# A hybrid diffusion block on eight cores: a second norm taken tile by tile inside the output projection, paired adaLN units, and six smaller moves

## The chip, the cores and the metric

The kernel runs on the 8 NeuronCores of one Trainium2 chip. The cores don't talk to each other: each takes two context sequences and half of a latent sequence. Time is device time in microseconds of the slowest core; lower is better.

## The reference, cut to what matters

One layer with model width D = 2048, 8 heads with values of 128, and a feed-forward width of 4 D:

```python
sh1, sc1, g1, sh2, sc2, g2 = split(silu(c) @ w_ada + b_ada)   # c_ctx for context tokens
h = rms_norm(x, w1) * (1 + sc1) + sh1
q, k, v, u, g = split(h @ w_in)          # q, k normed per 64; rotary on latent tokens
a = softmax(q1 k1) - lam * softmax(q2 k2)
att = rms_norm(a @ v, subln_w) * (1 - lam_init)
sgu = gelu(u) * (w_s @ layer_norm(gelu(g)) + b_s)   # 128x128 mixing per group and chunk
x = x + g1 * (concat(att, sgu) @ w_o)
h = rms_norm(x, w2) * (1 + sc2) + sh2    # the second norm
x = x + g2 * (square(relu(h @ w_ff1)) @ w_ff2)
```

Latent queries attend to all 2048 latent keys of their sequence and 256 cached context keys, context queries to their own 256. Outputs are both token streams and the new keys and values of the context.

## The kernel before, in words

A core owns 1536 tokens, in 12 tiles of 128: tiles 0 to 3 are context, 4 to 11 latent. Tiles 12 to 19 are the other half of its latent sequence, for keys and values alone. A scheduler, `Sched.add`, keeps readers and writers of each named buffer and puts semaphore waits in; an engine does its instructions in the order in which the program emits them. GpSimd's queue issues the weight loads (they convert to bf16), SP's the loads and stores of x and the small constants.

**Front (lines 300 to 460).** Twelve tiles are normed and transposed, and 16 slabs of adaLN weights (shift and scale of the first norm; `ada1_dma`, `ada1_mm`) go through a ring of four buffers. Slab by slab (`acc0`) the first four projection blocks of head 0 build up. Then head 0 is filled (`fill(0)`), with the other half's tiles normed, transposed and modulated in between by the generator `oth_gen` (L817). Its first three loads wait for `("sa1", 12)`. The bias load of `badaT_t` is emitted ahead of them on SP's queue; its buffer overlays the ring of the 16 slabs.

**Attention (L858 to L894).** 8 heads of 38 steps. A step: two exponentials on ScalarE (L866), some units of the next head's fill, the scores of the next step (`s_mm`, L739), and the value matmuls (L885). A fill has 13 projection blocks of 8 units and one cache unit; for heads 1 to 7 each of the 8 q and k blocks is followed by an adaLN unit (`ada_unit`), one of 64 slabs of 128 columns. 56 stand in the fills, 8 in head 7's steps (`si % 4 == 2`). The first 32 give the second norm's shift and scale with the slab as the stationary side (L513, 2 columns stream, result 128 x 2). The 32 gate units have the slab as the moving side (L531, result 2 x 128), load a bias row and store a piece of a row to the DRAM tensor `gate_rows`. All of it uses one PSUM tile, `pm`, shared with the q/k norm's sum (L554), the key transposes (L579), the cache transposes (L661) and the transposes of the finished block (L796); `pm_use` emits the pending reader of pm before its next writer. Two clocks, `FP` for fills and `MP` for finished blocks, post work so many ticks ahead. After the last step both are flushed.

**Weights of head 1** ("W" in `order`) are asked for after the first block of `fill(0)`.

**u, g and the mix.** u (L955): 8 slabs, three groups of 512 tokens each, into `sguT` through gelu. g (L982, `g_tile`): 12 tiles, with gelu, layer norm (square root on ScalarE, so table loads) and the mix (L1007), which runs two tiles behind. The last two mixes, `late_mix`, stand in the first slab of the output projection, after its second and its fourth group.

**Halves (L1062 on).** Two halves of six tiles. Output projection: 8 column blocks `nb`, each one 16 x 256 weight slab in a ring `wb` of three, six groups of 16 matmuls (L1073). `fused_add` multiplies by the gate (L1058) and adds into `acc` (L1059), both on VectorE; ScalarE squares into partial sums (L1080). When all 48 groups are done, the second norm: `norm_a` (sum, square root, reciprocal, a scaling of the 2048-wide row, L1093), `norm_b` (16 transposes, L1104, and copies on ScalarE and VectorE, L1111 and L1113) and `modulate` (12 scalings on VectorE, L1124, 4 on ScalarE, L1121, for tiles 0 to 3 and for 4 and 5). The first feed-forward group waits for all 16 of tiles 0 to 3. Then four rounds of ff1 (L1145) and ff2 (L1162), 8 slabs each. In the last round of half 0, SP stores each column block and then loads the next half's x into the same place, before the stores of the next block:

```python
for i, (dst, a_, n_) in enumerate(ytile(half, nb)):
    A("sp", ..., key=("yout", nb, i))
if half == 0:
    A("sp", ... dma_start(out=acc[:, :, nb * 256:nb * 256 + 256], in_=rows(xtile(nb))),
      writes=[("acc", ti, nb) for ti in range(6)], key=("xin", nb))
```

Of the kernel before, what the change touches and what calls it, by code (L numbers as in the profile page):

```python
# [8 lines left out]
F32 = mybir.dt.float32  # L9
# [4 lines left out]
D = 2048  # L14
# [128 lines left out]
def build_program():  # L143
# [10 lines left out]
    cT = din("cT", [128, 32]); w_adaA = din("w_adaA", [16, 128, 16 * 256]); badaA = din("badaA", [128, 64]); w_adaB = din("w_adaB", [64, 128, 16 * 128]); badaT = din("badaT", [128, 64]); badaG = din("badaG", [2, 2, D])  # L154
# [28 lines left out]
def _body(nc, top, L):  # L183
    globals().update({k: v for k, v in L.items() if k not in ("nc", "top")})
    with top:
# [32 lines left out]
        nw2_t = sbt(top, "nw2_t", [128, 16])  # L218
        attT = sbt(top, "attT", [128, 8, NTOK], BF16)
# [23 lines left out]
        with ExitStack() as pf:  # L243
# [6 lines left out]
            ARENA = 50700  # L250
            arena = sbt(pf, "arena", [128, ARENA], BF16)
            if True:
# [21 lines left out]
                badaT_t = ar.take(64, F32)  # L274
# [5 lines left out]
                wa2 = Ring("wa2", [tk3(16, 128) for i in range(3)])  # L280
                mch = Ring("mch", [ar.take(128, F32)[0:2, :] for i in range(2)])
# [219 lines left out]
                def ada_unit():  # L501
# [3 lines left out]
                    ada_i[0] += 1  # L505
                    ci, j = k // 16, k % 16
                    wt, wr = ada_slots.pop(k)
                    if ci < 2:
                        dst = S2 if ci == 0 else A2

                        def mm(e):
                            for kc in range(16):
                                ins = e.matmul(pm[:, 0:2], lhsT=wt[:, kc, :], rhs=scT[:, kc, :], start=(kc == 0), stop=(kc == 15))  # L513
                            return ins
                        pm_use(lambda: A("pe", mm, reads=[wr, "scT"], writes=[pmr]),
                               lambda: A("dve", lambda e: e.tensor_tensor(out=dst[:, j, :], in0=pm[:, 0:2], in1=badaT_t[:, ci * 32 + 2 * j:ci * 32 + 2 * j + 2], op=ALU.add),
                                         reads=[pmr, "badaT_t"], writes=[("modc2", ci, j)]))
                        if k == 31:
                            def fin():
                                for r in range(2):  # L520
                                    A("dve", lambda e, r=r: e.scalar_tensor_tensor(out=A2[:, :, r], in0=A2[:, :, r], scalar=1.0, in1=nw2_t[:], op0=ALU.add, op1=ALU.mult),
                                      reads=[("modc2", 1, jj) for jj in range(16)] + ["nw2_t"], writes=[("modc2", 1, jj) for jj in range(16)])
                            FP.post(4, fin)
# [741 lines left out]
```

How the kernel before makes its waits and increments, by code:

```python
    def _wait(self, eng, sem_name, sem, val):  # L39
        if self.waited[eng].get(sem_name, 0) >= val:
            return
        self.eng[eng].wait_ge(sem, val)
        self.waited[eng][sem_name] = val
# [1 line left out]
    def add(self, eng, fn, reads=(), writes=(), key=None):  # L45
# [15 lines left out]
        ins = fn(self.eng[eng])  # L61
        node = _Node()
        node.eng = eng
        node.dma = key is not None
        if key is not None:
            name = "d_" + str(key)
            if name not in self.dsem:
                self.dsem[name] = self.es.enter_context(self.nc.semaphore(name))
                self.dcnt[name] = 0
            self.dcnt[name] += 1
            ins.then_inc(self.dsem[name], 16)
            node.signal = (name, self.dsem[name], 16 * self.dcnt[name])
        else:
            self.cnt[eng] += 1
            ins.then_inc(self.esem[eng], 1)
            node.signal = ("c_" + eng, self.esem[eng], self.cnt[eng])
        for r in reads:
            self.readers.setdefault(r, []).append(node)
```

## Time and profile before

| | us |
|---|---|
| median of 3 runs (2758.24 to 2761.27) | 2758.82 |
| the profiled execution | 2762.95 |
| its span on the slowest core, core 3 | 2761.7 |
| TensorE busy | 2511.8 (91%) |
| VectorE busy | 988.5 (36%) |
| ScalarE busy | 839.6 (30%) |
| GpSimd busy | 210.2 (8%) |
| mean granted TensorE clock, core 3 | 0.972 |

The profile is of one execution, on the slowest core. Busy is the time in which an engine had an instruction of its own. The granted clock is that of TensorE as a share of 2.4 GHz; 0.50 is 1.2 GHz. A timeline merges neighbouring instructions of one line and tile. Matmuls overlap, so a row's duration reaches some 0.1 us or more into the next row.

### The profile page before, as it was taken

What the parts mean: (1) busy time and instruction counts of PE and PEld (TensorE: products, weight loads), DVE (VectorE), ACT (ScalarE), POOL (GpSimd) and SP (SyncE); (2) the same over time, 40 slices, a digit from 0 to 9 for tenths busy, and PEclk for the clock granted to TensorE, in tenths of its full rate; (3) what the DMA queues carried; (4) which work ended last, traced back from release to release, by engine and by line L of the source; (5) the groups of instructions that cost most, each with busy time, mean ns of one, the idle gap of its engine ahead of it and who ended that gap; (6) DMA issues with size and microseconds to landing.
All of it is one profiled execution on the core that took longest, in us unless ns stands there. A gap on an engine that the chain in (4) does not pass through costs nothing.

```text
span 2761.7 us, 57540 instructions; the slowest of 8 cores (2743.7 to 2761.7 us)
## 1 busy us (share of the span) xinstructions
PE 2511.8 (91%) x22176; PEld 1776.4 (64%) x22176; DVE 988.5 (36%) x2447; ACT 839.6 (30%) x1685; POOL 210.2 (8%) x338
## 2 busy tenths in 40 slices
PE   1458999999998889988999999999989999999999
PEld 1345565565565544467687786867875776868768
DVE  1334443443343320565142241423443331413324
ACT  2335665665665541643101101010122001010010
POOL 0111111111111000000000000000000000000000
PEclk9969999999999999998999999999998999999999
DMA  9994334334423355154555555557983555555556
GB/s 201 187 213 84 63 64 77 62 56 76 73 46 57 62 106 107 22 138 77 92 101 99 107 98 102 104 98 134 174 181 62 104 98 106 98 102 107 95 110 149
DMA packets 82298, 282.43 MB, mean 102 GB/s; under 512 B 11632, under 2 KB 45040, under 8 KB 58480
## 3 DMA queue, kind: packets, MB, share of 16 engines
q0 software_dynamic: 43232, 226.87, 47.4%
q1 hardware_dynamic: 38800, 51.89, 5.9%
q8 instruction: 182, 2.98, 0.4%
q14 instruction: 84, 0.69, 0.1%
HBM read 488.78 MB, written 16.81 MB: 183 GB/s over the span
## 4 chain that ended last, share of the span: by engine, by line
PE 80%; DMA 6%; DVE 5%; ACT 4%; issue 4%; DVEq 0%; ACTq 0%; SPq 0%; POOLq 0%; POOL 0%
PE pg L1145 8%; PE pS L1145 8%; PE pO L1162 8%; PE pS L1162 8%; PE pg L1162 8%; PE pO L1145 8%; PE pO L885 5%; PE pg L623 4%; PE pS L739 3%; PE pg L640 2%; PE pT L623 2%; DMA arena<-xp 2%; PE pO L1073 2%; PE pS L1073 2%; PE pg L1073 2%
## 5 line engine op out<-in xcount | busy, mean ns | idle before, releaser
L866 ACT ACTIVATE arena<-pS 128x512 bf16<-128x512 f32 x578 | 312.9, 593 | 245.5 <-PE pS L739 239.5
L1150 DVE TENSOR_TENSOR arena<-arena 128x512 bf16<-128x512 bf16 (+1 forms) x256 | 91.9, 359 | 572.2 <-ACT arena L1149 572.2
L1059 DVE TENSOR_TENSOR hT_own<-hT_own,arena 128x256 f32<-128x256 f32 x480 | 204.3, 426 | 63.5 <-DMA hT_own<-xs 12.0
L885 PE MATMUL pO<-arena 128*128 128x129 bf16 x2432 | 198.1, 225 | 11.5 <-ACT arena L866 9.0
L885 PEld LDWEIGHTS pO<-arena 128*128 128x128 bf16 x2432 | 144.9, 100 | 76.2 <-issue 75.9
L1145 PE MATMUL pg<-arena 128*128 128x256 bf16 (+1 forms) x960 | 157.5, 322 | 0.0
L1145 PE MATMUL pO<-arena 128*128 128x512 bf16 (+1 forms) x896 | 157.0, 333 | 0.0
L1162 PE MATMUL pS<-arena 128*128 128x256 bf16 x1344 | 153.6, 273 | 0.0
L1162 PE MATMUL pO<-arena 128*128 128x256 bf16 x1344 | 153.6, 273 | 0.0
L1162 PE MATMUL pg<-arena 128*128 128x256 bf16 x1344 | 153.6, 273 | 0.0
L1149 ACT ACTIVATE arena<-pg 128x512 bf16<-128x512 f32 (+1 forms) x86 | 42.4, 493 | 351.3 <-PE pg L1145 351.3
L1149 ACT ACTIVATE arena<-pS 128x256 bf16<-128x256 f32 (+1 forms) x86 | 42.0, 488 | 348.7 <-PE pS L1145 348.7
L1149 ACT ACTIVATE arena<-pO 128x512 bf16<-128x512 f32 (+1 forms) x84 | 41.2, 491 | 345.0 <-PE pO L1145 345.0
L1162 PEld LDWEIGHTS pO<-arena 128*128 128x128 bf16 x1344 | 131.4, 98 | 15.4
L1162 PEld LDWEIGHTS pg<-arena 128*128 128x128 bf16 x1344 | 131.4, 98 | 15.3
L1162 PEld LDWEIGHTS pS<-arena 128*128 128x128 bf16 x1344 | 131.3, 98 | 15.4
L1145 PE MATMUL pS<-arena 128*128 128x256 bf16 (+1 forms) x832 | 136.0, 322 | 0.0
L1145 PEld LDWEIGHTS pg<-arena 128*128 128x128 bf16 x960 | 93.9, 98 | 59.1
L1145 PEld LDWEIGHTS pO<-arena 128*128 128x128 bf16 x896 | 87.7, 98 | 63.9
L623 PE MATMUL pg<-hT_own,arena 128*128 128x512 bf16 x464 | 121.5, 389 | 0.0
L739 PE MATMUL pS<-arena 64*128 64x256 bf16 x1156 | 115.9, 279 | 4.7 <-ACT arena L866 4.2
L1145 PEld LDWEIGHTS pS<-arena 128*128 128x128 bf16 x832 | 81.4, 98 | 50.8
(236 smaller groups left out, 3755.9 us busy)
## 6 DMA issues: line engine op xcount, KB each, us to landing
arena<-w_ff POOLq DMA_DIRECT2D x84, 1024.0 KB, 8.9
shr<-w_ff POOLq DMA_DIRECT2D x44, 1024.0 KB, 9.0
arena<-w_adaB POOLq DMA_DIRECT2D x64, 512.0 KB, 5.5
arena<-w_adaA POOLq DMA_DIRECT2D x16, 1024.0 KB, 21.6
arena<-xs SPq DMA_DIRECT2D x16, 1024.0 KB, 9.7
arena<-w_in POOLq DMA_DIRECT2D x32, 512.0 KB, 8.0
arena<-w_o POOLq DMA_DIRECT2D x12, 1024.0 KB, 11.5
hT_own<-xs SPq DMA_DIRECT2D x8, 768.0 KB, 12.3
```

What stands on the lines that cost most here:

```text
L623: ins = e.matmul(pt[:], lhsT=wt[:, kc, :], rhs=hTs(kc, tb * 512, 512), start=(kc == 0), stop=(kc == 15))
L640: ins = e.matmul(pt[:, u * 128:(u + 1) * 128], lhsT=hTs(kc, tb * 512 + u * 128, 128), rhs=wt[:, kc, :], start=(kc == 0), stop=(kc == 15))
L739: ins = e.matmul(bk[c][:, j * 256:j * 256 + 256], lhsT=kT[p][64 * c:64 * c + 64, (kt + j) * 128:(kt + j) * 128 + 128], rhs=qz[p][64 * c:64 ...
L866: A("act", lambda e, t=bk[c], P=P: e.activation(out=P, in_=t[:], func=AF.Exp, scale=0.125), reads=[bkr[c]], writes=[Pr])
L885: ins = e.matmul(pO[b][:, c * 130:c * 130 + 129], lhsT=Ps[c][0][:, j * 256 + b * 128:j * 256 + b * 128 + 128], rhs=vv[p][:, kt + j, 0:129] ...
L1059: A("dve", lambda e: e.tensor_tensor(out=acc[:, ti, c], in0=acc[:, ti, c], in1=tmp, op=ALU.add), reads=[tmr, ("acc", ti, nb)], writes=[("a ...
L1073: ins = e.matmul(pt[:, 0:256], lhsT=lt, rhs=wcol(wt, kc, 0, 256), start=(kc == 0), stop=(kc == 15))
L1145: ins = e.matmul(pt[:, 0:cn], lhsT=wcol(wt, kc, fj * 128, 128), rhs=h2T[:, kc, c0:c0 + cn], start=(kc == 0), stop=(kc == 15))
L1149: A("act", lambda e, pt=pt, rl=rl, cn=cn: e.activation(out=rl[:, 0:cn], in_=pt[:, 0:cn], func=AF.Relu), reads=[pr], writes=[rlr])
L1150: A("dve", lambda e, rl=rl, fc=fc, c0=c0, cn=cn: e.tensor_tensor(out=aT[:, fc, c0:c0 + cn], in0=rl[:, 0:cn], in1=rl[:, 0:cn], op=ALU.mult) ...
L1162: ins = e.matmul(pt[:, 0:256], lhsT=aT[:, fc, ti * 128:(ti + 1) * 128], rhs=wcol(wt, fc, 0, 256), start=(fc == 0), stop=(fc == 15))
```

## The change

- adaLN units come in pairs, after every second q or k block of a fill, and in head 7 at steps 4, 10, 16 and 22. All 64 have the slab as the stationary side. Gates collect in `gcol`, are transposed once and stored in one DMA. The slab ring has four buffers.
- The flush after the last attention step goes; its posted steps run during u, two ticks of each clock per group. `wsb` and `bsb` are loaded after u's fourth slab.
- The late mixes stand after the fifth group of the first and of the second slab of the output projection.
- The second norm of tile ti - 1 runs beside the nb 6 and nb 7 groups of tile ti, for which two weight slabs are held. Square root and reciprocal become Ln and Exp. The first feed-forward group is in four quarters, each waiting for four of the 16 rows, with the last two tiles' transposes between quarters. For nb 6 and 7 the add of `fused_add` is on GpSimd.
- In the last round of half 0, x of block nb - 1 is loaded after the stores of block nb. The last store is three.
- The other half's first loads wait for `("sa1", 14)`; the weights of head 1 are asked for after k3.

```diff
-                        for kc in range(16):
-                            ins = e.matmul(pm[0:2, 0:128], lhsT=scT[:, kc, :], rhs=wt[:, kc, :], start=(kc == 0), stop=(kc == 15))
...
+                        for u in range(2):
+                            for kc in range(16):
+                                ins = e.matmul(pm[:, 2 * u:2 * u + 2], lhsT=sl[u][0][:, kc, :], rhs=scT[:, kc, :], start=(kc == 0), stop=(kc == 15))
...
+                    for kk in (k + 4, k + 5):
+                        if kk < 64:
+                            FP.post(4, lambda kk=kk: ada_dma(kk))
...
-                        order = ["v1", "W", "v2", "v0", "C", "k0", "q0", "k3", "v3", "k4", "V", "v4"]
+                        order = ["v1", "v2", "v0", "C", "k0", "q0", "k3", "W", "v3", "k4", "V", "v4"]
...
-                            yield from ada(1)
+                            nb_ += 1
+                            if nb_ % 2 == 0:
+                                yield from ada(1)
...
-                FILL_UNITS = 8 * 13 + 1 + 8
+                FILL_UNITS = 8 * 13 + 1 + 4
...
-                    ld = [x_load(t, reads=[("sa1", 12)]) for t in range(12, 15)]
+                    ld = [x_load(t, reads=[("sa1", 14)]) for t in range(12, 15)]
...
-                        if si % 4 == 2:
+                        if si % NS in (4, 10, 16, 22):
                             ada_unit()
...
-                MP.flush()
-                FP.flush()
-                while ada_i[0] < 64:
-                    ada_unit()
-                    FP.flush()
...
+                    for _ in range(2):
+                        MP.tick()
+                        FP.tick()
...
+                if gi == 3:
+                    MP.flush()
+                    FP.flush()
...
+                for nb in range(6):
+                    wt, wr = pend_w.pop(0)
+                    for ti in range(6):
+                        o_group(nb, ti, wt, wr)
+                        if late_mix and ti == 4:
+                            late_mix.pop(0)[1]()
+                    w_more()
...
+                w67 = [pend_w.pop(0), pend_w.pop(0)]
+                na = {}
                 for ti in range(6):
...
+                    o_group(6, ti, *w67[0])
+                    if ti >= 1:
+                        norm_a1(ti - 1)
+                    if ti >= 2:
+                        norm_b(ti - 2, *na[ti - 2])
                     if ti == 5:
                         modulate(0)
...
+                    o_group(7, ti, *w67[1])
+                    if ti >= 1:
+                        na[ti - 1] = norm_a2(ti - 1)
+                norm_a1(5)
+                na[5] = norm_a2(5)
+                w_more()
+                w_more()
+                tail_norm = [lambda: norm_b(4, *na[4]), lambda: norm_b(5, *na[5]), lambda: modulate(1)]
...
+                            if rd == 0 and fb == 0 and c0 == 0 and fj == 0:
+                                for k4 in range(0, 16, 4):
...
+                                    A("pe", mm4, reads=[wr] + [("h2T", kc, 0) for kc in range(k4, k4 + 4)], writes=[pr])
+                                    if k4 in (4, 12):
+                                        tail_norm.pop(0)()
+                                tail_norm.pop(0)()
...
-                                A("sp", lambda e, nb=nb: e.dma_start(out=acc[:, :, nb * 256:nb * 256 + 256], in_=rows(xtile(nb))),
-                                  writes=[("acc", ti, nb) for ti in range(6)], key=("xin", nb))
+                                for n1 in ([nb - 1] if nb else []) + ([7] if nb == 7 else []):
...
```

## Rows read from the trace of the kernel before

**Rows 1.** Section 2 of the page: TensorE's busy tenths in 40 slices of the span.
```profile
PE   1458999999998889988999999999989999999999
```

**Rows 2.** Stretches: length, busy us (instructions) of PE, PEld, DVE, ACT, POOL, clock, DMA share, GB/s.
```profile
1186.00:1211.00 25.00, 15.70 (x116) 12.29 (x114) 18.80 (x39) 9.66 (x22) 0.00 (x0) 0.80 0.85 253
...
1284.00:1314.00 30.00, 18.66 (x133) 12.46 (x131) 21.12 (x51) 14.25 (x25) 0.53 (x1) 0.72 0.19 36
1892.00:1976.00 84.00, 84.00 (x772) 75.28 (x771) 40.43 (x96) 0.38 (x1) 4.24 (x8) 1.00 0.87 164
1976.00:2059.00 83.00, 83.00 (x763) 74.40 (x761) 36.62 (x87) 21.39 (x84) 4.23 (x8) 1.00 0.91 185
2059.00:2095.00 36.00, 20.52 (x133) 13.58 (x131) 24.48 (x60) 16.32 (x33) 0.53 (x1) 0.62 0.20 43
```

**Rows 3.** TensorE's groups by line, 235 to 1008: count, busy us, mean ns, idle before.
```profile
L531 PE MATMUL pT<-arena,scT 128*2 128x128 bf16 x512 | 36.6, 225 | 5.8 <-ACT arena L591 4.1 <-ACT arena L558 1.0
...
L554 PE MATMUL pT<-arena,bones 128*128 128x512 bf16 x56 | 21.9, 392 | 29.4 <-DVE arena L535 10.8 <-DVE st_b L765 6.1 <-DVE S L516 5.6
L513 PE MATMUL pT<-scT,arena 128*128 128x2 bf16 x512 | 17.4, 163 | 7.5 <-ACT arena L591 5.5 <-DMA arena<-w_adaB 1.0
```

**Rows 4.** TensorE's timeline in attention: start, duration, [idle before].
```profile
444.06 0.38 PE L554 MATMUL pT<-arena,bones 128*128 128x512 bf16 x1 [0.52 <-DVE arena L790]
...
455.63 0.54 PE L513 MATMUL pT<-scT,arena 128*128 128x2 bf16 x16
...
458.52 0.38 PE L554 MATMUL pT<-arena,bones 128*128 128x512 bf16 x1 [1.01 <-DVE A L516]
...
859.12 1.09 PE L531 MATMUL pT<-arena,scT 128*2 128x128 bf16 x16
```

**Rows 5.** TensorE's timeline from the end of attention into u.
```profile
1012.77 0.37 PE L796 MATMUL pT<-identb,arena 128*128 128x128 bf16 x2 [4.97 <-DVE arena L790]
1012.97 9.91 PE L955 MATMUL pg<-hT_own,arena 128*128 128x512 bf16 x32
1022.72 7.07 PE L955 MATMUL pS<-hT_own,arena 128*128 128x512 bf16 x32
```

**Rows 6.** TensorE's timeline at the start of the output projection.
```profile
1201.23 0.38 PE L1007 MATMUL pS<-arena 128*128 128x128 bf16 x4 [2.49 <-DVE arena L1058]
1204.95 0.58 PE L1007 MATMUL pS<-arena 128*128 128x128 bf16 x4 [3.34 <-DVE arena L1058]
```

**Rows 7.** The second norm of half 0 on three engines, in their timelines.
```profile
1293.38 1.10 PE L1104 MATMUL pT<-identb,arena 128*128 128x128 bf16 x16 [1.07 <-DVE arena L1093]
...
1286.92 1.29 DVE L1093 TENSOR_SCALAR arena<-hT_own,st_a 128x2048 bf16<-128x2048 f32 x1 [0.17 <-DVE st_a L1092]
...
1301.78 3.96 DVE L1124 TENSOR_SCALAR arena<-arena,A,S 128x512 bf16<-128x512 bf16 x12
...
1300.84 2.91 ACT L1121 ACTIVATE arena<-arena,S,A 128x512 bf16<-128x512 bf16 x4
```

**Rows 8.** GpSimd's rotary products and VectorE beside one of them.
```profile
191.99 1.94 POOL L586 TENSOR_TENSOR arena<-arena 128x512 f32<-128x512 bf16 x1 [6.31 <-DVE arena L565]
...
289.15 1.03 POOL L586 TENSOR_TENSOR arena<-arena 128x512 f32<-128x512 bf16 x1 [6.42 <-ACT arena L866]
...
289.13 1.08 DVE L767 TENSOR_SCALAR st_b<-st_b,neglam 128x2 f32<-128x2 f32 x1
```

**Rows 9.** VectorE's wait for x in half 1, and section 6 of the page.
```profile
2061.20 0.43 DVE L1059 TENSOR_TENSOR hT_own<-hT_own,arena 128x256 f32<-128x256 f32 x1 [9.84 <-DMA hT_own<-xs]
...
arena<-w_ff POOLq DMA_DIRECT2D x84, 1024.0 KB, 8.9
```

**Rows 10.** SP's queue: bias load, the other half's tiles, the last stores.
```profile
170.75 0.33 SPq L815 DMA_DIRECT2D arena<-badaT  x1
171.27 30.69 SPq L300 DMA_DIRECT2D arena<-xs  x7
...
2747.39 10.86 SPq L1169 DMA_DIRECT2D ys<-hT_own  x2
```

More of the change, by code:

```diff
@@ L279, in _body @@
                 vv.append(tk3(22, 130))
-                wa2 = Ring("wa2", [tk3(16, 128) for i in range(3)])
-                mch = Ring("mch", [ar.take(128, F32)[0:2, :] for i in range(2)])
+                wa2 = Ring("wa2", [tk3(16, 128) for i in range(4)])
                 o_raw = [tk3(4, 130, F32) for c in range(2)]
@@ new lines, in ada_unit, with tr, out @@
+                    if k == 62:
+                        def tr():
+                            A("pe", lambda e: e.transpose(pm[0:64, 0:128], gcol[:], identf[:]),
+                              reads=[("modc2", c_, jj) for c_ in (2, 3) for jj in range(16)] + ["identf"], writes=[pmr])
+                        def out():
+                            A("dve", lambda e: e.tensor_copy(out=grow[:], in_=pm[0:64, 0:128]), reads=[pmr], writes=["grow"])
+                            A("sp", lambda e: e.dma_start(out=gsc.rearrange("g (j c) -> (g j) c", c=128), in_=grow[:]), reads=["grow"],
+                              writes=[("gsc", g, jj) for g in range(2) for jj in range(16)], key="gsc")
+                        FP.post(4, lambda: pm_use(tr, out))
@@ L854, in _body @@
                 A("dve", lambda e: e.memset(vv[1][:, :, 128:130], 1.0), writes=[("vones", 1)])
-                for k in range(3):
+                for k in range(4):
                     ada_dma(k)
@@ L1083, in _body, with norm_a1 @@
-                if half == 0:
-                    S.seed([("h2T", k_, b_) for k_ in range(16) for b_ in range(2)] + [("aT", k_, b_) for k_ in range(16) for b_ in (0, 512)] + [("xn2", 0), ("xn2", 1)],
-                           S.nodes([("wg", i) for i in range(4)] + [("gg", i) for i in range(2)] + [("gn", i) for i in range(3)] + [("mt", i) for i in range(3)] + ["sgw", "wsb", "bsb"]))
-                def norm_a(ti):
-                    sa, sar = st_a.next()
+                nsa = {}
+                def norm_a1(ti):
+                    sa, sar = nsa[ti] = st_a.next()
+                    A("dve", lambda e: e.reduce_sum(out=sa[:, 0:1], in_=ssp[:, ti * 8:ti * 8 + 8], axis=mybir.AxisListType.X), reads=[("ssp", ti, nb) for nb in range(8)], writes=[sar])
+                    A("act", lambda e: e.activation(out=sa[:, 1:2], in_=sa[:, 0:1], func=AF.Ln, bias=epsc[:, 0:1], scale=1.0 / D), reads=[sar, "epsc"], writes=[sar])
+                    A("act", lambda e: e.activation(out=sa[:, 2:3], in_=sa[:, 1:2], func=AF.Exp, scale=-0.5), reads=[sar], writes=[sar])
@@ L1089, in norm_a, with norm_a2 @@
+                def norm_a2(ti):
+                    sa, sar = nsa[ti]
                     xn, xnr = xn2_ring.next()
[L1090 to L1092 removed]
```

128 lines of the change are left out of this document (59 added, 69 removed).

## The prediction

> **What bounds the kernel now.** I read the digits of TensorE's busy share first [rows 1]: from the 24th of the 40 slices to the end nearly all are 9, with dips in the 30th and 31st. In the stretches around the gaps the granted clock is 0.62 to 0.80, in the full ones 1.00 [rows 2]. So the second half of the span is worth only its gaps, and each gap costs twice, once as idle time and once as matmuls at the lower level of 1.2 GHz. The stretches give the sizes [rows 2]: 25 us around the first output projection hold 15.7 us of work; the two second norms take 30 us and 36 us; between them TensorE is busy throughout. Attention is the third place. TensorE is busy for about 690 of 770 us there, so work removed from it is time, and its idle time stands mostly before the small matmuls that share one PSUM tile, pm: 29.4 us before L554 alone [rows 3]. ScalarE and VectorE are busy for less than two thirds of that stretch and bind only for moments.
>
> The profiled execution took 2762.95 us (span 2761.7 and 1.3 around it). That is 4.1 over the median of the three runs shown, 2758.8. I subtract the terms from the median.
>
> **Paired adaLN units.** 64 units stand in attention. The first 32 (L513) print 0.54 us for their 16 matmuls, the 32 gate units (L531) print 1.09 [rows 4], since they stream 128 columns instead of 2. The change makes all 64 of the first kind. 24 gate units lie in heads that TensorE bounds: 24 x 0.55 = 13 us. The other 8 lie in the last head, where each step also waits for its exponentials; of 8 x 0.55 = 4.4 us I take 3.5 (bounds 0 and 7; 7 if the slow-clock stretches there go too).
>
> Pairing halves how often pm is held. I do not count half of the waits, though. In a head with mod units the waits are 0.5 us after k1's unit, 0.4 at the cache transposes after q1's, about 1.0 each after k2's, q2's and k4's, and 1.4 before q0's unit [rows 3, 4], of which one of two sizes stands there. The pair now comes after every second block, so after k2, q2, k4 and q0: exactly where the long waits are. What goes is the 0.5 and the 0.4, near 0.8 us a head with the hand-over: 7 heads, 5 us. Bounds: 0, and half of the 29.4, 15. The SP queue loses 64 small DMAs and VectorE 32 small adds of 0.28; nobody waits for either. The gate rows leave in one DMA after a transpose, 200 us before they are read. Slabs of two pairs are loaded ahead (four buffers), 5.5 us each against some 26 us between pairs, so nothing is late. Attention together: 13 + 5 + 3.5 = 21.5.
>
> **The end of attention under u.** TensorE waits 4.97 us for the last block's norm and then runs the first two u groups in 9.75 us, which later take 6.9 [rows 5]. The u slabs are there before, so u can start behind the last value matmul: 4.97 + 0.2 + 2.8 = 8.0. The left-over steps run in u's slots, with two table loads more on ScalarE, which is idle for four fifths of that stage. I take 7.5; bounds 4 (the clock starts low anyway) and 8.2. The loads of wsT and the bias move behind u's fourth slab, some 25 us later; their first reader comes 70 us after, and what is queued behind them on GpSimd (output weights and gates) is wanted later still.
>
> **The first output groups.** The mix of tile 10 stood after the second group, that of tile 11 after the fourth; waits of 3.5, 2.5 and 3.3 us (the last two in [rows 6]) come from g's chain of ScalarE and VectorE, which runs 5 us late and cannot be moved. 25 us hold 11.8 of full-clock work (6 groups of 1.75 and three mixes of 0.44): 13.2 lost. With the mixes after the fifth group of the first and second slab, TensorE still waits for the same PSUM release (2.9), does three groups, then waits about 3 for VectorE, and loses 2 to 2.5 at the low clock: about 8.5 lost. Gain 4.5, bounds 2 and 7.
>
> **The second norm.** Full-clock work in each window of [rows 2] is six transposes (1.10 printed for 16, 0.9 from start to start) and two groups of 512, 6.9 [rows 5, 7]: 12.3. So 17.7 is lost in half 0 and 23.7 in half 1. Half 1's extra 6 comes from x: the last column block's load is late, and VectorE waits 9.84 us for it [rows 9]. SP had held each load until the stores before it landed. Now a load is issued one slab behind its stores, so the last leaves some 15 us after half 0 ends instead of 75, and this wait goes whole.
>
> After the change, per tile: two groups (3.5) and one transpose set (0.9), 4.4 us of TensorE. VectorE needs two multiplies, a reduce, a scaling of 1.29 [rows 7] and a copy, 3.0: covered. The scaling ends 2.1 us after the nb 7 group whose multiply stands before it; the transposes come 1.75 after: 0.35 wait in each of four tiles, 1.5. Then the corner, counted from the end of the fifth nb 7 group: the sixth ends at 4.8; ScalarE's copy of tile 3 ends near 5.8, the 12 scalings of modulate take 3.96 and ScalarE's four 2.9 [rows 7], so the first quarter group starts at 6.9, not 4.8 (2.1 idle). VectorE is free at 9.8, then multiplies, then scales tile 4 until 11.6, and the transposes of tile 4 stand in front of TensorE from 8.9 (2.7 idle). Tile 5 still needs its GpSimd add, square and scaling, so its transposes end near 16.9. Of these 12.1 us 5.3 are work: 6.8 lost, and 2 more at the low clock. With the 1.5: 10.3 a half, 20.6 for both. Gain 41.4 - 20.6 = 20.8; bounds 14 (clock low throughout the corner) and 27 (only the first idle stretch stays).
>
> **A GpSimd add** of 128x256 has no row. The nearest is its 128x512 product, 1.03 [rows 8]; half of that is the lower bound and 1.94, the longest such row, the upper. I take 0.8, nearest to the usual row. On its path it costs only in the corner. There the row that matters is VectorE's: a scaling of two elements takes 1.08 us where it starts with a GpSimd product of 1.03 [rows 8]; one waited for the other. The Trainium skill (SBUF — State Buffer, Who interferes with whom) calls the shared ports an exclusive lock for copy and tensor_scalar on VectorE against any GpSimd instruction, and the trace agrees. By that rule the last add waits for tile 4's scaling; without it the corner would be 1.3 us shorter, and the sum 2.6 larger. My 16.9 already holds that wait, as a case of two instructions that start together in [rows 8].
>
> **The end** [rows 10]: the last store leaves at 2757.9 and the span ends 3.8 later. As three stores, the last one a sixth of the size, near the 2.3 of the smallest stores: 1.4; bounds 0.5 and 2.
>
> **Nothing for these.** The tile loads at slab 14: they leave at 171.27, right behind the bias load at 170.75 [rows 10], which waits for the last slab's matmuls at 170.7. SP is in order, so neither gate bound, and this edit does nothing. Head 1's weights later: they free the DMA engines at 172 to 186, when ScalarE is the one late, and load them at 194 to 205, when it still is: 0, bounds -3 and +2. Two output weights held at once: the next slab but one is asked for only after the last add; a load takes 8.9 us [rows 9] and the first feed-forward slab covers some 19. Ln and Exp in place of square root: one table load a half, before the first tile's scaling, beside output groups.
>
> **Sum.** 21.5 + 7.5 + 4.5 + 20.8 + 1.4 = 55.7, so 2758.8 - 55.7 = 2703. All lower ends together give 2728, and all upper ones 2683 (the upper end of attention taken at 30).
>
> **Rivals.** (a) Weights late at the turn of the halves. The DMA engines are 0.87 and 0.91 busy in the two stretches there [rows 2], some 149 us of work in 167, of which 16 slabs at 5.9 are 95 and stores and loads of x the rest, 6.7 a slab. Closed up, a slab of ff2 has 12.6 us of traffic in 10.5 of matmuls. SP's share may be taken from weights: up to 8 x 2.1 = 17 us, 2720. Against it, a weight may be 20 us under way before it is missed. (b) The norm hides less: short idle stretches keep the clock at its lower level through nb 6 and 7, so 21 us in each half take up to 42. At a quarter of that, 2714; whole, 2745. (c) Attention's waits go as well as the work, 10 us more, and the first idle stretch alone stays at the corner, 6 more: 2687. (d) Slower than before: GpSimd's adds bind. 24 adds stand in series with the norm, two per 4.4 us, so from 2.2 us an add TensorE runs at their pace, and from 2.2 + 55.7 / 24 = 4.5 us the kernel is slower; at 5 us it is 2771. The longest row, 1.94 for twice the elements, speaks against it. (e) The parts do not do what they say: the pair keeps all waits, x still comes late and the corner costs as before. 13 to 20 us would stay, 2740; it needs several of my readings wrong.
>
> **Numbers.** A measurement of this kernel tells about 0.2%, 5.5 us, from no change. Forecast, 2690 to 2718: 0.58. (a) and (b), 2718 to 2745: 0.20. (c), under 2690: 0.13. (e): 0.04. No change: 0.02. (d): 0.03. The range 2684 to 2730 leaves out the farther half of (a) and (b), a little of (c), and the last three. Faster 0.95, same 0.02, slower 0.03.
>
> **What would show it.** L531 gone and about 34 us of L513 matmuls; waits at L554 still near 1 us, about three a head; u's first group straight behind the last value matmul at full clock; one idle stretch less before the second slab of the output projection; no DMA wait on VectorE in half 1's adds; idle stretches of about 2 and 3 us within the first feed-forward group of each half, alike in both; tile loads issued at the same time as before. Wrong would be GpSimd adds over 2 us, a clock of 0.5 in nb 6 and 7, weight waits on TensorE near the turn of the halves, or waits for exponentials in heads 0 to 6.

## The result, and the profile after

The changed kernel takes 2726.61 us (median of 3, 2725.70 to 2728.21) against 2758.82. The ratio is 0.9882, 95% interval 0.9859 to 0.9904: 32.2 us or 1.2% faster. The forecast was 2703, so the time lies inside the range and the direction was right, but only 32 of the 55.7 us came. In some executions, whatever the kernel, the cores of one die or of both show a lower granted clock and the time is longer; these are left out of all ratios, ranges and profiles below, and where a median holds one it moves it by 1.4 us at most.

The profiled execution took 2728.21 us. The page of the kernel after, its busy times and digits:

```profile
span 2727.2 us, 57310 instructions; the slowest of 8 cores (2708.5 to 2727.2 us)
PE 2498.4 (92%) x22177; PEld 1761.0 (65%) x22177; DVE 967.3 (35%) x2380; ACT 844.3 (31%) x1700; POOL 234.6 (9%) x362
PE   1458999999999889998999999999999999999999
```

Against [rows 1], the 8 in the 30th slice has gone (the second norm of half 1; the 31st, which the prediction names too, is a 9 in both rows), and so has that in the 18th, the start of the output projection. Those in attention have hardly thinned out: 14th and 15th for 13th to 15th.

I then cut both traces into stages, at the first instruction of each stage (heads at the first of their exponentials), and took the mean over the eight cores:

| stage, us | before | after | gained | forecast |
|---|---|---|---|---|
| front | 235.0 | 236.8 | -1.8 | 0 |
| heads 0 to 6 | 701.3 | 694.0 | 7.3 | 18.0 |
| head 7 and u | 158.5 | 150.3 | 8.2 | 11.0 |
| g | 87.3 | 87.4 | -0.1 | 0 |
| half 0, output projection to the end of the first ff1 round | 204.6 | 193.7 | 10.9 | 11.9 |
| half 1, the same | 190.8 | 182.3 | 8.5 | 13.4 |
| the other ff rounds, in each half | 585.0 | 585.0 | 0 | 0 |
| end | 4.9 | 3.8 | 1.1 | 1.4 |
| sum of gains (differences from rounding) | | | 34.1 | 55.7 |

Half of the missing 21.6 us is in heads 0 to 6. The work went there as forecast. TensorE's groups by line, core 3 of the kernel after, 237 to 1008 us:

```profile
L517 PE MATMUL pT<-scT,arena 128*128 128x2 bf16 x1024 | 30.3, 163 | 5.9 <-ACT arena L593 5.9
L556 PE MATMUL pT<-arena,bones 128*128 128x512 bf16 x57 | 23.0, 404 | 42.2 <-DVE gcol L520 13.4 <-DVE A L520 8.9 <-DVE S L520 8.9
```

The two adaLN lines of [rows 3], 54.0 us busy, have become 30.3: 23.7 us of work less. But the idle time before the q/k norm's sum (L554 before, L556 now) rose from 29.4 to 42.2 us, and what ends most of it is L520, the adaLN unit's own add on VectorE. And TensorE's clock is low more often. The same stretch of both kernels on the slowest core of each, 7 and 3 (length, busy us of PE, PEld, DVE, ACT, POOL, then granted clock, DMA share, GB/s), after and before:

```profile
240.00:930.00 690.00, 635.74 (x7376) 400.63 (x7373) 267.09 (x716) 422.03 (x828) 97.28 (x132) 0.96 0.37 66
```

```profile
240.00:930.00 690.00, 637.02 (x7360) 404.93 (x7358) 273.91 (x740) 420.81 (x825) 94.82 (x128) 0.98 0.38 65
```

Summed from the clock records of all cores, attention holds 43.0 us at the 1.2 GHz level in the mean core before and 78.5 us after. Of the 35.5 us more, 13.0 are in heads 0 to 6 and 22.5 in the last head. TensorE's timeline shows one place in heads 0 to 6, core 3, kernel after:

```profile
282.56 0.94 PE L517 MATMUL pT<-scT,arena 128*128 128x2 bf16 x32
283.44 0.39 PE L744 MATMUL pS<-arena 64*128 64x256 bf16 x4
283.76 0.63 PE L890 MATMUL pO<-arena 128*128 128x129 bf16 x8
...
287.25 0.38 PE L556 MATMUL pT<-arena,bones 128*128 128x512 bf16 x1 [2.42 <-DVE S L520]
...
288.74 0.61 PE L744 MATMUL pS<-arena 64*128 64x256 bf16 x4
289.28 1.05 PE L890 MATMUL pO<-arena 128*128 128x129 bf16 x8
290.12 2.17 PE L642 MATMUL pg<-arena,shr 128*128 128x128 bf16 x24
```

The pair's 32 matmuls end at 283.5; L556 wants the same PSUM tile, and waits 2.42 us for the pair's add. Behind it the scores print 0.61 instead of 0.39 and the value matmuls 1.05 instead of 0.63, for about 3 us. VectorE's timeline over the same wait shows why the add is late:

```profile
284.27 0.76 DVE L765 COPY arena<-pO 128x258 f32<-128x258 f32 x2 [2.50 <-PE pO L890]
285.13 0.18 DVE L770 RECIPROCAL st_b<-arena 128x4 f32<-128x4 f32 x1
285.42 0.23 DVE L772 TENSOR_SCALAR st_b<-st_b,neglam 128x2 f32<-128x2 f32 x1
285.56 0.68 DVE L603 TENSOR_TENSOR arena<-pg,arena 128x512 f32<-128x512 f32 x1
286.34 0.69 DVE L607 TENSOR_TENSOR arena<-arena 128x512 bf16<-128x512 f32 x1
286.95 0.15 DVE L520 TENSOR_TENSOR S<-pT,arena 128x4 f32<-128x4 f32 x1
```

VectorE itself had been idle for 2.50 us. Then the copies out of pO and q1's last two rotary steps (L603, L607) come first, and the 0.15 us add stands behind them in program order. Before, a single unit stood between q1 and q2; each unit is one tick of the fills' clock. q1's last step is due 11 ticks after its block. With the tick gone, it is emitted between the matmuls of the pair behind q2 and the pair's add; before, it was emitted ahead of the unit's matmuls and was done when the add came. VectorE's timeline there, core 3, kernel before:

```profile
280.53 0.69 DVE L601 TENSOR_TENSOR arena<-pg,arena 128x512 f32<-128x512 f32 x1 [2.15 <-PE pg L583]
281.32 0.69 DVE L605 TENSOR_TENSOR arena<-arena 128x512 bf16<-128x512 f32 x1
...
283.65 0.15 DVE L516 TENSOR_TENSOR S<-pT,arena 128x2 f32<-128x2 f32 x1
```

The bones matmul (L554) starts at 283.95, after a wait of 1.02 us.

### The profile page after: what moved, and what is told of

Its sections match the earlier page's. It is cut to its first block, busy times and chain, and to the rows that moved or that the text cites. A ratio compares the mean times of both kernels' runs of the same rounds, so it can differ in the third digit from the quotient of the medians.

```text
span 2727.2 us, 57310 instructions; the slowest of 8 cores (2708.5 to 2727.2 us)
## 1 busy us (share of the span) xinstructions
PE 2498.4 (92%) x22177; PEld 1761.0 (65%) x22177; DVE 967.3 (35%) x2380; ACT 844.3 (31%) x1700; POOL 234.6 (9%) x362
## 4 chain that ended last, share of the span: by engine, by line
PE 82%; ACT 5%; DMA 5%; DVE 4%; issue 3%; POOL 0%; DVEq 0%; ACTq 0%; SPq 0%; POOLq 0%
PE pS L1195 8%; PE pO L1195 8%; PE pg L1195 8%; PE pg L1167 8%; PE pS L1167 8%; PE pO L1167 8%; PE pO L890 5%; PE pg L625 4%; PE pS L744 3%; PE pg L642 2%; PE pT L625 2%; DMA arena<-xp 2%; PE pS L1123 2%; PE pO L1123 2%; PE pg L1123 2%
## 5 line engine op out<-in xcount | busy, mean ns | idle before, releaser
L890 PE MATMUL pO<-arena 128*128 128x129 bf16 x2432 | 204.6, 230 | 10.1 <-ACT arena L871 6.7
L1066 DVE TENSOR_TENSOR hT_own<-hT_own,arena 128x256 f32<-128x256 f32 x456 | 193.9, 425 | 51.5 <-DVE arena L1065 6.8
L1182 ACT ACTIVATE arena<-pg 128x512 bf16<-128x512 f32 (+1 forms) x86 | 42.4, 493 | 345.1 <-PE pg L1167 345.1
## 6 DMA issues: line engine op xcount, KB each, us to landing
arena<-w_adaA POOLq DMA_DIRECT2D x16, 1024.0 KB, 21.6
```

Of the source, the lines that this page charges most:

```text
L890: ins = e.matmul(pO[b][:, c * 130:c * 130 + 129], lhsT=Ps[c][0][:, j * 256 + b * 128:j * 256 + b * 128 + 128], rhs=vv[p][:, kt + j, 0:129] ...
L1066: A(eng, lambda e: e.tensor_tensor(out=acc[:, ti, c], in0=acc[:, ti, c], in1=tmp, op=ALU.add), reads=[tmr, ("acc", ti, nb)], writes=[("acc ...
L1182: A("act", lambda e, pt=pt, rl=rl, cn=cn: e.activation(out=rl[:, 0:cn], in_=pt[:, 0:cn], func=AF.Relu), reads=[pr], writes=[rlr])
```

## The experiments

"Measured" is the median, ratios are to the kernel before, timed beside it; "mean" is the mean span of the eight cores in the profile, 2718.5 for the kernel after.

**1. The form against the grouping.** One slab per unit again, a unit after every block as before, but gate units in the new form too.

```diff
-                    ada_i[0] += 2
+                    ada_i[0] += 1
...
-                            if nb_ % 2 == 0:
-                                yield from ada(1)
+                            yield from ada(1)
...
-                        if si % NS in (4, 10, 16, 22):
+                        if si % 4 == 2:
```

> The changed kernel with single adaLN units after every q and k block (as before), all with the slab as the stationary side. Theory: the form of the matmuls gives 0.55 us per gate unit, and the pairs give nothing or lose, since the small adds on VectorE now stand behind a finished block's work and the clock falls after each such wait. Then heads 5 to 7 take about 99.0 us each as the mod heads did before, heads 1 to 4 are as before (96 to 99), and the kernel is within 3 us of the changed one. Rival (my prediction): pairing itself saves 0.7 us a head; then this kernel is about 5 us slower.

Measured 2722.29, ratio 0.9844 (0.9822 to 0.9867). Heads 0 to 6 take 689.6, idle time before L556 is 31.0 on core 3, and the low clock fills 70.0 us of attention. So pairing, as the change places it, is worth nothing; it costs some 4 us (694.0 less 689.6 in heads 0 to 6; the intervals of the two ratios overlap a little).

**2. The pair after the odd blocks** (k1, q1, k3, k0 instead of k2, q2, k4, q0).

```diff
-                            if nb_ % 2 == 0:
+                            if nb_ % 2 == 1:
```

> The changed kernel with the pairs after the first, third, fifth and seventh q or k block (k1, q1, k3, k0) in place of the second, fourth and so on. Theory: the wait of 2.4 us at the bones matmul after q2's pair and the 1.0 us waits come from the place of the pair against the finished block's work on VectorE; moved, idle time at that matmul falls from 42 us to 30 or less, one low-clock stretch a head goes, and heads take 1.5 to 3 us less each: about 10 to 15 us faster, 2714. Rival: the low clock in attention comes from the 32 matmuls of two columns themselves, wherever they stand; then the low stretches stay at two a head and the gain is under 5 us.

Measured 2680.02, ratio 0.9696 (0.9678 to 0.9714), mean 2672.6: 46 us better than the change, by a single digit. Heads 0 to 6 take 649.5 instead of 694.0. The low clock fills 35.0 us of attention, 30.7 of them in the last head, and none in heads 1 to 6 on any core. TensorE's groups by line, core 3 of this kernel, the same stretch:

```profile
L517 PE MATMUL pT<-scT,arena 128*128 128x2 bf16 x1024 | 30.3, 163 | 3.2 <-DMA arena<-w_adaB 2.4
L556 PE MATMUL pT<-arena,bones 128*128 128x512 bf16 x56 | 21.1, 377 | 10.3 <-ACT arena L551 9.3 <-issue 0.2
```

The same 1024 matmuls take the same 30.3 us, so in heads 1 to 6 it isn't the two-column matmuls themselves that bring the clock down. The idle time before L556 fell from 42.2 to 10.3, and no add of VectorE is among its releasers. TensorE's timeline there, the place that answers to the one above:

```profile
267.71 0.94 PE L517 MATMUL pT<-scT,arena 128*128 128x2 bf16 x32
269.07 0.27 PE L663 MATMUL pT<-identb,arena 128*128 128x128 bf16 x2 [0.42 <-DVE S L520]
...
270.10 0.38 PE L556 MATMUL pT<-arena,bones 128*128 128x512 bf16 x1
```

**3. The pair's add emitted a tick earlier.** If only its place in VectorE's order counts, this should do as much.

```diff
+                    hold = pm_held[0]
+                    FP.post(1, lambda: pm_free() if pm_held[0] is hold else None)
```

> The changed kernel with the pair's add on VectorE emitted at the next unit and not just before the bones matmul. Theory: that matmul waits because the add is emitted late and stands behind other work of VectorE; emitted one unit earlier, before the value block's copies, idle time there falls from 42 us to 20 or less and the gain is 10 to 20 us. Rival: VectorE reaches the add no earlier since it waits in order for the same things; then idle time and total are unchanged within 3 us.

Measured 2725.33, ratio 0.9858 (0.9836 to 0.988), heads 0 to 6 at 693.4, idle time before the bones matmul (L558 in this kernel) at 42.4. Nothing moved: the add was now due in the very tick in which q1's last step is due, and behind it. The edit did not do what it was for, so it decides only that one tick is too little.

**4. Ticks without units.** Pairs stay after the even blocks; after the odd ones an empty unit keeps the fills' clock as before.

```diff
                             if nb_ % 2 == 0:
                                 yield from ada(1)
+                            elif h > 0:
+                                tick()
+                                yield
...
-                FILL_UNITS = 8 * 13 + 1 + 4
+                FILL_UNITS = 8 * 13 + 1 + 8
```

> The changed kernel with pairs where they are, and an empty unit (a tick of the fill's clock, no work) after each q or k block that has no pair, so that the posted steps fall as they did before the change. Theory: the 2.4 us wait after q2's pair comes from the tick that went: q1's rotary steps, 11 ticks after q1, now come due ahead of the pair's add. With the tick back that wait is about 1.0 us, idle time at the bones matmul falls from 42 to about 30 us, and heads 0 to 6 take 2 us less each: 2712. Rival: the place alone decides and the ticks don't; then heads take 99 us as in the changed kernel, and only the odd places (92 us) avoid it.

Measured 2719.78, ratio 0.9846 (0.9814 to 0.9877); heads 0 to 6 686.8. TensorE's timeline on core 3, after q2's pair:

```profile
282.68 0.55 PE L556 MATMUL pT<-arena,bones 128*128 128x512 bf16 x1 [1.02 <-DVE S L520]
...
284.86 0.61 PE L747 MATMUL pS<-arena 64*128 64x256 bf16 x4
285.40 0.98 PE L893 MATMUL pO<-arena 128*128 128x129 bf16 x8
```

The 2.42 us wait is 1.02 now, and all idle time before L556 on core 3 is 31.4. So the lost tick explains this wait, and putting it back is worth about 7 us of the kernel. (The empty units also take slots of their own, since the fill is spread over 113 units instead of 109; the two are not separated.) It doesn't explain the other 37 us to experiment 2. A wait of 1 us is still followed by slow matmuls here, and heads 0 to 6 still hold 41.7 us at the low clock, so the place of the pair, not the tick, is what decides. The mean core's idle time of TensorE (waits over 0.15 us), and the part of it before the bones matmul (both 240 to 880 us), beside its time at the low clock:

| kernel | all idle, us | before L556 | low clock, heads 0 to 6 | low clock, last head |
|---|---|---|---|---|
| before | 49.9 | 24.1 | 30.1 | 12.9 |
| after | 53.0 | 30.6 | 43.1 | 35.4 |
| 1, single units | 52.2 | 26.1 | 35.2 | 34.8 |
| 4, empty units | 50.5 | 23.5 | 41.7 | 41.9 |
| 3, early add | 53.3 | 30.7 | 40.5 | 37.1 |
| 2, odd blocks | 25.7 | 8.6 | 4.3 | 30.7 |

The low clock goes with the longer waits. In heads 1 to 6, all cores together, the kernel after has 48 waits of TensorE over 1.3 us, and 40 of them were soon followed by a low stretch; of its 88 waits of 0.9 to 1.3 us 25 were. Experiment 2 has no wait of 0.9 us there.

What each part takes comes out when a stage is split in three: idle time, work at full clock (TensorE's busy time, with what ran at 1.2 GHz counted half) and the other half, which is the price of the clock. Mean core:

| us | idle | work | clock | in all |
|---|---|---|---|---|
| heads 0 to 6, before | 57.8 | 630.0 | 13.6 | 701.3 |
| after | 59.5 | 615.1 | 19.4 | 694.0 |
| 2, odd blocks | 30.3 | 617.3 | 1.9 | 649.5 |
| last head, before | 23.7 | 44.3 | 5.3 | 73.3 |
| after | 15.8 | 36.4 | 15.1 | 67.4 |
| 9, old flush | 21.0 | 36.9 | 15.1 | 72.9 |

So of the 44.5 us between the change and experiment 2, 29.2 are idle time and 17.5 the clock, against 2.2 more of work.

**5. The front's two edits undone.**

```diff
-                        order = ["v1", "v2", "v0", "C", "k0", "q0", "k3", "W", "v3", "k4", "V", "v4"]
+                        order = ["v1", "W", "v2", "v0", "C", "k0", "q0", "k3", "v3", "k4", "V", "v4"]
...
-                ld = [x_load(t, reads=[("sa1", 14)]) for t in range(12, 15)]
+                ld = [x_load(t, reads=[("sa1", 12)]) for t in range(12, 15)]
```

> The changed kernel with its two front edits undone (head 1's weights asked for after v1, the other half's first tiles let in at slab 12). Theory: the front is bound by ScalarE and by the x tiles of all eight cores sharing memory; asking for head 1's weights later moves 2 MB of reads into the loads of tiles 15 to 19 and costs 1 to 3 us. Then this kernel is 1 to 3 us faster than the changed one (about 2724), and the mean start of attention over the cores is back at 235 from 236.8. Rival: the 3.5 us between the slowest cores' starts is scatter from run to run; then there is no difference within 1 us and the starts scatter over 230 to 241 again.

Measured 2721.43, ratio 0.9861 (0.9824 to 0.9898), mean 2716.6. The front takes 234.6, and 234.5 and 233.6 in experiments 11 and 12, which hold the same edit; in the ten traces with the new front it takes 235.3 to 237.3. So the new front costs 2 us. SP's queue in the kernel after speaks against the gate as the part that costs:

```profile
170.47 0.33 SPq L820 DMA_DIRECT2D arena<-badaT  x1
171.00 1.71 SPq L300 DMA_DIRECT2D arena<-xs  x3
```

The tile loads leave at 171.00, right behind the bias, as in [rows 10]. The later weights of head 1 are what is left; no run undoes them alone, and none shows that the eight cores share the memory, as the expectation has it.

**6. All adds on VectorE.**

```diff
-fused_add(pt, pr, ti, nb, 0, r, "pool" if nb >= 6 else "dve")
+fused_add(pt, pr, ti, nb, 0, r, "dve")
```

> The changed kernel with the adds of column blocks 6 and 7 on VectorE as before. Theory: a GpSimd add takes 0.72 us alone and 1.63 beside a scaling, on the path only in the corner of each half; VectorE then has 0.43 us more per group but has room (3.9 of 4.4 us a tile), and the corner's last square comes 1.2 us sooner. Then this kernel is within 3 us of the changed one, faster by up to 2. Rival (the move was needed): VectorE is full beside the norm, the transposes wait over 1 us in each tile, and it is 5 us or more slower.

Measured 2728.13, ratio 0.9863 (0.9783 to 0.9942). Output projection 101.8 and 91.2, first ff1 rounds 90.7 and 90.6, against 102.1, 90.2, 89.8 and 90.3. From the first output group to the end of the ff1 round that is 193.7 and 183.1, against 193.7 and 182.3: nothing in half 0, 0.8 us in half 1.

**7. The late mixes early again** (in the first column block, after tiles 1 and 3).

```diff
-                        if late_mix and ti == 4:
+                        if late_mix and ti in (1, 3):
```

> The changed kernel with both late mixes back in the first slab of the output projection, after its second and fourth group. Theory: moving them gives 4.5 us, so this kernel is 3 to 6 us slower and the first stretch of half 0 takes 106 us from the first group to the last of the slabs, not 102. Rival: the same PSUM releases bind either way and the difference is under 2 us.

Measured 2726.52, ratio 0.9864 (0.9799 to 0.9929). The output projection of half 0 takes 104.0 instead of 102.1: 1.9 us.

**8. x loaded behind its own block's stores again.**

```diff
-                    for n1 in ([nb - 1] if nb else []) + ([7] if nb == 7 else []):
+                    for n1 in [nb]:
```

> The changed kernel with each column block's x asked for right behind its own stores, as before. Theory: only the core whose last x load is late is hit; one or a few cores wait 5 to 10 us before nb 7 of half 1, the others nothing, and the slowest core's time is 2 to 6 us longer. Rival: every core waits and it is 6 us or more in all; or none does on this chip and there is no difference.

Measured 2727.65, ratio 0.9863 (0.9758 to 0.9967), no difference to the change, and in its trace, one execution, VectorE waits for x on no core. In the trace of before, the wait of 9.84 us [rows 9] is on core 3 alone: 12.0 us over three waits there, 0.5 on core 7.

**9. The old flush at the end of attention.**

```diff
+                MP.flush()
+                FP.flush()
                 assert ada_i[0] == 64
```

> The changed kernel with the flush of the posted steps back at the end of attention. Theory: u's first matmul waits again for the last block's norm, 5 us, and the clock falls for some 7 us: from the start of head 7 to the start of g it takes 7.5 us more (158 against 150). Rival: head 7's low clock hides a part, 4 us or less.

Measured 2731.65, ratio 0.9882 (0.9817 to 0.9947), mean 2725.1 against 2718.5. Head 7 takes 72.9 instead of 67.4 and u 84.4 instead of 82.9: 7.0 us.

**10. Ln and Exp called once ahead of time,** in half 0's fourth column block, on a value that nobody reads, so that the table load falls there.

```diff
+                        if half == 0 and nb == 3 and ti == 5:
+                            A("act", lambda e: e.activation(out=warm[:, 0:1], in_=epsc[:, 0:1], func=AF.Ln), reads=["epsc"], writes=["warm"])
+                            A("act", lambda e: e.activation(out=warm[:, 1:2], in_=epsc[:, 0:1], func=AF.Exp), reads=["epsc"], writes=["warm"])
```

> The changed kernel with one Ln and one Exp on a constant after the fourth output slab of half 0, so that ScalarE's table is loaded before the first tile's norm (nothing of the result changes). Theory: the 2.2 us wait before tile 0's transposes in half 0, and the low clock behind it on most cores, come from that table load; the wait falls to 0.9 or less, and the stretch from the first output group to the last falls from 102.1 to about 99 us, 3 us off the whole. Rival: the wait comes from the chain of the first norm itself; the stretch stays at 102 (half 1 shows what is left without a load: 90.2 with no such wait).

Measured 2723.16, ratio 0.9857 (0.9819 to 0.9895), mean 2715.2. The output projection of half 0 takes 99.7 instead of 102.1. TensorE's timeline at tile 0, the kernel after first (core 7), then this one (core 0):

```profile
1260.37 1.11 PE L1092 MATMUL pT<-identb,arena 128*128 128x128 bf16 x16 [2.21 <-DVE arena L1081]
1261.27 1.91 PE L1123 MATMUL pO<-arena,attT 128*128 128x256 bf16 x8
```

```profile
1258.22 1.05 PE L1092 MATMUL pT<-identb,arena 128*128 128x128 bf16 x16 [1.07 <-DVE arena L1081]
1259.11 1.04 PE L1123 MATMUL pO<-arena,attT 128*128 128x256 bf16 x8
```

The wait is 1.14 shorter, and the matmuls behind it no longer run at half speed (1.91 after, where the usual print is 1.04).

**11. The version that the runs point to:** experiments 2, 5 and 10 in one kernel.

> Pairs after the odd blocks, the front's two edits undone, and the table loaded early. Theory: the parts add up, 44 + 2 + 3 us under the changed kernel: about 2676. Rival: the front's 2 us is scatter, 2679.

Measured 2674.67, ratio 0.9684 (0.9652 to 0.9715), mean 2669.0, front 234.5, heads 0 to 6 at 650.3. It is the fastest kernel of this study, 84 us faster than before, though only 5 us from experiment 2.

**12. On top of it, the corner of the second norm filled otherwise:** two ff1 groups over tiles 0 to 3 in quarters, and the norms of tiles 4 and 5 spread over both.

```diff
-                                    if k4 in (4, 12):
+                                    if (fj, k4) in ((0, 12), (1, 8)):
```

> The kernel before this one with the last two tiles' transposes moved: tile 4's behind the whole first feed-forward group, tile 5's behind three quarters of the second. Theory: TensorE no longer stands at tile 4's transposes with ready quarters behind them, the 2.3 us idle stretch goes in both halves and with it the low clock: 2 to 3 us a half, 4 to 6 in all, about 2671. Rival: modulate of the last two tiles comes later, so the wait moves to the third group (512 to 768) and the gain is under 2 us.

Measured 2677.44 (2675.52 to 2677.46), ratio 0.9695 (0.9649 to 0.9741), mean 2670.8. The first ff1 rounds take 91.3 in both halves, 1.3 longer. TensorE's timeline at the corner, core 2:

```profile
1230.27 1.05 PE L1092 MATMUL pT<-identb,arena 128*128 128x128 bf16 x16 [0.40 <-DVE arena L1081]
...
1234.05 1.09 PE L1092 MATMUL pT<-identb,arena 128*128 128x128 bf16 x16
...
1239.35 5.24 PE L1170 MATMUL pS<-arena,shr 128*128 128x256 bf16 x32 [3.35 <-DVE arena L1112]
```

The waits before the transposes are 0.40 and none, but the third group then waits 3.35 us for the scalings of tiles 4 and 5. VectorE starts these 11.3 us behind its scalings of tiles 0 to 3, and 11.8 behind in experiment 11 (core 2 of both): hardly earlier. The corner's length is VectorE's, and the order on TensorE says where it is paid. The rival of the expectation came.

## Why the prediction was right in direction and half right in size

2726.6 lies in the range of 2684 to 2730, but not in the band of 2690 to 2718 that had 0.58. It lies in the band of rivals (a) and (b), and neither came. The sum of all lower ends was 2728, so the time was inside thanks to the width of the range more than to the sum: that part is luck.

**Paired units: the failed step.** "What goes is the 0.5 and the 0.4, near 0.8 us a head" took the waits of [rows 3, 4] as fixed to their places. They are not: the ticks of the units set when VectorE's other steps are emitted, and taking one unit out between q1 and q2 put two rotary steps between the pair's matmuls and its add. That made 1.0 us into 2.42, and putting the tick back is worth 7 us (experiment 4). The clock is the second part. I had priced it where a whole stage stalls, in u and at the corner, and at nothing in heads 0 to 6, whose waits I took for half a microsecond or one each. By the table of three parts, the 18 us forecast for heads 0 to 6, 13 of work and 5 of waits, became 14.9 less work, 1.7 more idle time and 5.8 more for the clock: 7.3. By heads, 4 to 6, beside which the gate slabs run, gained 9.9 together, and heads 0 to 3 lost 2.5. Rival (c), attention's waits going as well, was the wrong way round for this change, and too small, at 10 us, for what placement can give: 44.5. I had seen that even blocks are "exactly where the long waits are", but read it as a reason for a small gain, not as a question to the neighbouring choice.

**Last head and u: the clock again.** 8.2 for 11.0. The flush measured 7.0 against 7.5. u starts where it was forecast, right behind the last value matmul (TensorE, kernel after):

```profile
1005.89 0.62 PE L890 MATMUL pO<-arena 128*128 128x129 bf16 x8 [0.69 <-ACT arena L871]
1006.35 7.07 PE L953 MATMUL pg<-hT_own,arena 128*128 128x512 bf16 x32
```

By difference, the eight gate units in the last head gave 1.2 for 3.5. The forecast took off a part of their 4.4 because each step waits for its exponentials, but idle time didn't grow: with the old flush (experiment 9) the last head has 2.7 us less of it than before and 7.4 less work, and the clock takes 9.8 more. The low clock there is 12.9 us before and 30.7 to 41.9 in all kernels with the new units, paired or single, with the new flush or the old one; no run undoes their form alone, so its cause stays open.

**First output groups.** Undoing this edit gives back 1.9, not 4.5. By difference, the stretch lost 13.0 before (98.3 less 84.0 of groups and 1.3 of mixes) and loses 8.2 now (102.1 less the same stretch of half 1, 90.2, the 2.4 of experiment 10 and the 1.3). The forecast said 13.2 and 8.7. So the two ends were right, and some 3 us of the gain belong to something else that isn't isolated here.

**Second norm: right where it was worked out.** Half 1 before, without core 3's wait, was 190.1; less the 17.7 lost, 172.4 of bare work. After, it is 182.3: 9.9 lost, for 10.3 forecast. The corner has the forecast's shape; TensorE's timeline, half 1, kernel after:

```profile
2043.30 1.05 PE L1092 MATMUL pT<-identb,arena 128*128 128x128 bf16 x16 [0.30 <-DVE arena L1081]
...
2047.88 1.99 PE L1173 MATMUL pS<-arena,shr 128*128 128x512 bf16 x8 [1.78 <-DVE arena L1112]
2052.21 1.06 PE L1092 MATMUL pT<-identb,arena 128*128 128x128 bf16 x16 [2.33 <-DVE arena L1081]
2053.10 3.58 PE L1173 MATMUL pS<-arena,shr 128*128 128x512 bf16 x8
```

0.30 us before a tile's transposes (forecast 0.35), 1.78 before the first quarter (2.1), 2.33 before tile 4 (2.7), and then 3.58 for eight matmuls that otherwise take 1.99, the low clock that I put at 2. The 172.4 leans on the prediction's own 17.7; split in three like attention, half 1 has 172.8 of work before and 173.4 after, and loses 8.9 after (7.1 idle and 1.8 for the clock), so the size holds within 1.4 us.

**"Ln and Exp in place of square root": the second failed step, small.** I costed the table load at nothing, "before the first tile's scaling, beside output groups". It is on that scaling's path. ScalarE at tile 0, half 0, kernel after:

```profile
1256.81 1.28 ACT L1075 ACT_TABLE_LOAD   x1
1258.11 0.29 ACT L1075 ACTIVATE st_a<-st_a,epsc 128x1 f32<-128x1 f32 x1
1258.49 0.20 ACT L1076 ACTIVATE st_a<-st_a 128x1 f32<-128x1 f32 x1
```

The scaling starts at 1258.94, directly behind. Experiment 10 takes the load away from there and gains 2.4 us, of which 1.14 is wait; the rest I put down to the clock. Half 1 needs no load and has only the 0.3 us waits.

**The x load: the third.** I subtracted 6 us for the 9.84 us wait from a median of other executions. The wait was real, on one core of one execution, the slowest. The mean over cores holds 0.7 us of it (190.8 against 190.1 without core 3), and nothing showed that the other executions, from whose median I subtracted, had it. Half 1 came 4.9 short of its forecast, all of it this term's, and experiment 8 shows no gain of the reordering that can be told.

**GpSimd's adds.** The median add is 0.73 (0.8 forecast), and the one beside a 1.28 us scaling is 1.63 (the one line's summary, then GpSimd's and VectorE's timelines, half 1, kernel after):

```profile
L1066 POOL TENSOR_TENSOR hT_own<-hT_own,arena x24: 718/727/1637, 1251.9 to 2051.0; 128x256 f32<-128x256 f32 x24
```

```profile
2051.01 1.63 POOL L1066 TENSOR_TENSOR hT_own<-hT_own,arena 128x256 f32<-128x256 f32 x1 [6.54 <-DVE arena L1065]
```

```profile
2050.79 1.28 DVE L1081 TENSOR_SCALAR arena<-hT_own,st_a 128x2048 bf16<-128x2048 f32 x1
```

The add began 0.22 us into the scaling and ended 0.57 behind it: it did most of its own work only when the scaling was over. By the rule of the Trainium skill (SBUF — State Buffer, Who interferes with whom), an exclusive lock, the trace agrees. Rival (d), adds over 4.5 us, had nothing to it.

**Front.** 0 was forecast, with bounds -3 and +2; it costs 2. The tile loads leave when they did, as forecast. The step that failed is then, by what is left, that ScalarE is late in any case when head 1's weights come. **End:** 1.1 for 1.4. **Weights at the turn of the halves**, rival (a): the other rounds take 585.0 before and after, so no weight is late. Rival (b), the norm's clock, did not come beyond the 2 us counted. Of rival (e), only the part on the pair's waits came; the corner cost what was forecast.

**What stays open.** Why the low clock comes 1.5 times a head (72 stretches in heads 1 to 6 of eight cores) with pairs at even blocks and never there at odd ones. The long waits and the low clock go together in experiment 2, so cause and companion are not separated, and why the waits are short there is shown for one place only. Why the last head holds so much more low clock than before is open too. A PSUM tile of its own for the pairs would tell; it wasn't tried.

## What to carry to other kernels

Work that is slotted between others by a clock of its own has two prices, its duration and its place, and here the place was worth 46 us where the work was worth 24; when you move or merge such units, list what the neighbouring engine has queued ahead of their last step, and try each slot. A wait on one core of one profiled execution belongs to that execution: before a term of it is taken off a median, look whether the other cores have it. A first use of a new activation function in a stage has a path of its own, so ask who waits for it.

## What the runs showed of the hardware

- Some waits of 1 to 2.4 us on TensorE inside a stage that is 92% busy were followed by stretches of 3 to 7 us at the 1.2 GHz level (0.39 becomes 0.61, 0.63 becomes 1.05), as behind 287.25 and 282.68 in two of the listings above. In heads 1 to 6 this holds for 40 of 48 waits over 1.3 us and for 25 of 88 of 0.9 to 1.3 us; without such waits (experiment 2) there was no low stretch. The Trainium skill (TensorE: Matmul & The Clock Gate, A second HAM failure mode: psum-queue depth-cycling) tells of a kernel whose short idle times between groups of matmuls made the clock go up and down. The traces here agree, at waits on one shared PSUM tile.
- In the last head the 1.2 GHz level filled 12.9 us before and 30.7 to 41.9 in every kernel whose gate units are two-column matmuls.
- A GpSimd add of 128x256 takes 0.73 us alone and 1.63 beside a VectorE scaling of 1.28.
- An activation table load took 1.28 us. With it moved out of the way the stage was 2.4 us shorter, 1.14 us of it as a shorter wait of TensorE; the matmuls behind that wait also ran at full clock again.
